# Delta rule: the two 64-token chunks of a block side by side, each on its own quarter of the array

## What is computed

```python
gc = jnp.cumsum(g, axis=-1)                       # within a chunk
decay = jnp.exp(jnp.where(causal, gc[..., :, None] - gc[..., None, :], -jnp.inf))
lower = jnp.where(strict, jnp.einsum('bhnid,bhnjd->bhnij', kb, k) * decay, 0.0)
tmat = lax.linalg.triangular_solve(eye + lower, ...)   # inverse of eye + lower, 64 x 64
u = jnp.einsum('bhnij,bhnjd->bhnid', tmat, v * beta[..., None])
w = jnp.einsum('bhnij,bhnjd->bhnid', tmat, kb * jnp.exp(gc)[..., None])
a_intra = jnp.where(causal, jnp.einsum('bhnid,bhnjd->bhnij', q, k) * decay, 0.0)
def step(S, inp):                                 # one chunk after another
    v_new = ui - wi @ S
    o = (qi * exp(gci)) @ S + ai @ v_new
    S = S * exp(glast) + (ki * exp(glast - gci)).T @ v_new
```

## Time and profile before

| | |
|---|---|
| runs | 3397.33, 3400.24, 3403.83 us |
| span of the profiled execution, first to last instruction | 3398.0 us |
| TensorE busy in the span | 3301.7 us (97%) |
| first pair: heads, inversion, state | 22.6, 30.2, 21.9 us |
| second pair: heads, inversion, state | 25.1, 31.7, 21.8 us |

### The profile page before, as it was taken

The page is one execution under the profiler, slowest core; times in us unless marked ns, Lnnn a source line. Parts: engine busy times, 40 slices in busy tenths (PEclk is TensorE's granted clock), DMA queues, the critical chain, the costliest instruction groups (busy, mean ns, idle before and its releaser), DMA issues. The chain is left out here.

```text
span 3398.0 us, 46483 instructions
## 1 busy us (share of the span) xinstructions
PE 3301.7 (97%) x18292; PEld 3053.0 (90%) x18292; DVE 2275.5 (67%) x3841; ACT 1235.4 (36%) x2071; POOL 80.7 (2%) x190
## 2 busy tenths in 40 slices
PE   8999999999999999989999999989999999999999
PEld 6999999988899999989999999977888888888777
DVE  5979896467677777787777766664333766466654
ACT  5111112256553433363433343543222432334432
POOL 0000000000000000000000000000000000000100
PEclk9999999999999999999999999999999999999999
DMA  5545553200132222232232221112233320122232
GB/s 209 186 168 180 191 176 110 73 26 26 42 88 67 87 87 79 90 84 65 73 100 87 93 87 61 44 61 87 94 100 95 124 63 20 54 78 74 69 100 94
DMA packets 95272, 313.57 MB, mean 92 GB/s; under 512 B 11424, under 2 KB 15712, under 8 KB 93520
## 3 DMA queue, kind: packets, MB, share of 16 engines
q1 hardware_dynamic: 88128, 290.04, 25.9%
q0 software_dynamic: 6928, 20.55, 2.2%
HBM read 300.06 MB, written 4.19 MB: 90 GB/s over the span
## 5 line engine op out<-in xcount | busy, mean ns | idle before, releaser
L669 PE MATMUL psum<-zh,wh 128*128 128x384 f32 (+2 forms) x2384 | 777.1, 371 | 24.3 <-DVE h L752 5.7
L639 ACT ACTIVATE wh<-raw 128x512 fp32r<-128x512 f32 (+3 forms) x551 | 447.4, 817 | 836.3 <-PE psum L669 431.9
L669 PE MATMUL psum<-zh,rawl 128*128 128x384 f32 (+2 forms) x2384 | 750.9, 360 | 0.0
L669 PE MATMUL psum<-zl,wh 128*128 128x384 f32 (+2 forms) x2372 | 747.6, 360 | 0.0
L649 DVE TENSOR_TENSOR rawl<-raw,wh 128x512 fp32r<-128x512 f32 (+3 forms) x551 | 502.6, 927 | 242.9 <-ACT wh L639 241.6
L669 PEld LDWEIGHTS psum<-zh,wh 128*128 128x128 f32 x2384 | 439.5, 190 | 79.5 <-issue 25.5
L1135 PE MATMUL psum<-formq,wh 128*128 128x386 f32 x1848 | 479.7, 341 | 10.9 <-DVE made_l L649 4.1
L669 PEld LDWEIGHTS psum<-zh,rawl 128*128 128x128 f32 x2384 | 441.2, 190 | 43.0
L669 PEld LDWEIGHTS psum<-zl,wh 128*128 128x128 f32 x2372 | 438.9, 190 | 41.5 <-issue 2.9
L1135 PEld LDWEIGHTS psum<-formq,wh 128*128 128x128 f32 x1848 | 337.5, 189 | 16.5 <-DVE made_l L649 5.0
L752 DVE SCALAR_TENSOR_TENSOR h<-psum,mod,h 128x512 f32<-128x512 f32 (+1 forms) x288 | 170.0, 627 | 190.7 <-PE psum L669 190.6
(11 more groups left out here) (494 smaller groups left out, 4747.7 us busy)
## 6 DMA issues: line engine op xcount, KB each, us to landing
raw<-in_wup SPq DMA_DIRECT2D x176, 512.0 KB, 4.1
modw<-in_mod_w SPq DMA_DIRECT2D x128, 512.0 KB, 3.7
raw<-in_w_sw SPq DMA_DIRECT2D x36, 512.0 KB, 3.6
raw<-in_wdn SPq DMA_DIRECT2D x64, 256.0 KB, 3.9
raw<-in_wdn SPq DMA_DIRECT2D x32, 448.0 KB, 3.2
adaw<-in_ada_w SPq DMA_DIRECT2D x8, 1024.0 KB, 15.0
raw<-in_wdn SPq DMA_DIRECT2D x16, 512.0 KB, 4.0
raw<-in_od_in SPq DMA_DIRECT2D x16, 512.0 KB, 3.6
```

Of the source, the lines that this page charges most:

```text
L639: nc.scalar.activation(hi_of(n, i), x, ACT.Copy).then_inc(w_hi, 1)
L669: last = nc.tensor.matmul(psum[:, at + to:at + to + e - s], w[:, q * P:(q + 1) * P], x[:, q, s:e], start=(q == 0 and j == 0), stop=(q == s ...
```

## The change

Wherever a matrix over pairs of tokens is block diagonal, only the two 64 by 64 chunks are kept: chunk 0 in partitions 0 to 63 and chunk 1 in partitions 64 to 127, both in columns 0 to 63 (`C`) of the same buffers. Each product becomes two (`for r in CHUNKS`), one for each chunk. In the inversion both operands and the result of a chunk lie in its own 64 partitions, so chunk 0 uses rows and columns 0 to 63 of TensorE's array and chunk 1 rows and columns 64 to 127. KK, KQ and BET contract over all 128 rows and write 64 output partitions each. The transpose of `uu` becomes a product with the identity. The w products write the two row halves into two banks (XB and UB), and ScalarE gathers them. ScalarE and VectorE work on 64 of 128 columns per head. `at_` stays 128 by 128; its zeros are set once. The mask constant keeps its size and is laid out anew. In `dn_head_pe` the row sums in chunk form are a further product, beside BET in the same bank.

```diff
@@ -3098,7 +3098,15 @@
             pool.wait_ge(n_sum, 7)
             pool.dma_start(dmask[:], t["c_dmask"]).then_inc(dmask_loaded, 16)
 
-        MASKT, CUM, BLK = dmask[:, 0, :], dmask[:, 1, :], dmask[:, 2, :]
+
+
+        C = slice(0, 64)
+        CHUNKS = (slice(0, 64), slice(64, 128))
+        CUM, BLK = dmask[:, 1, :], dmask[:, 2, :]
+        MASKT, IDENT = dmask[:, 0, C], dmask[:, 0, 64:128]
+
+        def level_mask(lv):
+            return mid(dmask[:, 3 + lv, C], 4)
 
...
@@ -3127,12 +3135,19 @@
                 w(dd, "lt", a - 1)
             for hd in range(4):
                 nc.tensor.matmul(bank4(ROW)[:, hd], buf["xx"][:, hd], CUM, start=True, stop=True)
-                last = nc.tensor.matmul(bank4(BET)[:, hd], buf["uc"][:, hd], ident[:], start=True, stop=True)
+            for hd in range(4):
+                for r in CHUNKS:
+                    nc.tensor.matmul(bank4(BET)[r, hd, 64:128], buf["xx"][:, hd, C], CUM[:, r], start=True, stop=True)
+                for r in CHUNKS:
+                    last = nc.tensor.matmul(bank4(BET)[r, hd, C], buf["uc"][:, hd, C], ident[:, r],
+                                            start=True, stop=True)
             last.then_inc(dp.sem, 1)
             for hd in range(4):
                 q, k = dn[:, hd, tok], dn[:, 4 + hd, tok]
-                nc.tensor.matmul(bank4(KK)[:, hd], k, k, start=True, stop=True)
-                last = nc.tensor.matmul(bank4(KQ)[:, hd], k, q, start=True, stop=True)
+                for r in CHUNKS:
+                    nc.tensor.matmul(bank4(KK)[r, hd, C], k[:, r], k[:, r], start=True, stop=True)
+                for r in CHUNKS:
+                    last = nc.tensor.matmul(bank4(KQ)[r, hd, C], k[:, r], q[:, r], start=True, stop=True)
             last.then_inc(dp.sem, 1)
             if a % 2:
                 w(dd, "vb", a - 1)
@@ -3151,7 +3166,9 @@
                 if a % 2 == 0:
                     w(dd, "et", a + 1)
                 for hd in range(4):
-                    last = nc.tensor.transpose(bank4(ROW + a % 2)[:, hd], dnbs[a % 2]["uu"][:, hd], ident[:])
+                    for r in CHUNKS:
+                        last = nc.tensor.matmul(bank4(ROW + a % 2)[r, hd, C], dnbs[a % 2]["uu"][r, hd, C], ident[r, r],
+                                                start=True, stop=True)
                 last.then_inc(dp.sem, 1)
             for lv in LV:
                 for a in pair:
@@ -3162,8 +3179,9 @@
                     else:
                         w(dd, f"tt{lv - 1}", a)
                     for hd in range(4):
-                        last = nc.tensor.matmul(bank4(XB[a % 2])[:, hd], buf["uc"][:, hd], buf["tt"][:, hd],
-                                                start=True, stop=True)
+                        for r in CHUNKS:
+                            last = nc.tensor.matmul(bank4(XB[a % 2])[r, hd, C], buf["uc"][r, hd, C],
+                                                    buf["tt"][r, hd, C], start=True, stop=True)
                     last.then_inc(dp.sem, 1)
                 for a in pair:
                     buf = dnbs[a % 2]
@@ -3171,21 +3189,26 @@
                     if lv > 1:
                         w(dd, f"tu{lv - 1}", a)
                     for hd in range(4):
-                        last = nc.tensor.matmul(bank4(UB[a % 2])[:, hd], buf["xx"][:, hd], buf["uu"][:, hd],
-                                                start=True, stop=True)
+                        for r in CHUNKS:
+                            last = nc.tensor.matmul(bank4(UB[a % 2])[r, hd, C], buf["xx"][r, hd, C],
+                                                    buf["uu"][r, hd, C], start=True, stop=True)
                     if lv < 5:
                         for hd in range(4):
-                            last = nc.tensor.matmul(bank4(TB[a % 2])[:, hd], buf["uu"][:, hd], buf["xx"][:, hd],
-                                                    start=True, stop=True)
+                            for r in CHUNKS:
+                                last = nc.tensor.matmul(bank4(TB[a % 2])[r, hd, C], buf["uu"][r, hd, C],
+                                                        buf["xx"][r, hd, C], start=True, stop=True)
                     last.then_inc(dp.sem, 1)
             for a in pair:
                 buf = dnbs[a % 2]
                 w(dd, "tu5", a)
                 for hd in range(4):
-                    nc.tensor.matmul(bank4(TB[a % 2])[:, hd], buf["uu"][:, hd], buf["vb"][:, hd],
-                                     start=True, stop=True)
-                    last = nc.tensor.matmul(bank4(XB[a % 2])[:, hd], buf["kbe"][:, hd], buf["uu"][:, hd],
-                                            start=True, stop=True)
+                    for r in CHUNKS:
+                        nc.tensor.matmul(bank4(TB[a % 2])[r, hd], buf["uu"][r, hd, C], buf["vb"][r, hd],
+                                         start=True, stop=True)
+                    for half in CHUNKS:
+                        for b, r in zip((XB, UB), CHUNKS):
+                            last = nc.tensor.matmul(bank4(b[a % 2])[half, hd, C], buf["kbe"][r, hd, half],
+                                                    buf["uu"][r, hd, C], start=True, stop=True)
                 last.then_inc(dp.sem, 1)
...
@@ -3269,19 +3292,20 @@
                     w(dp, "ws1", a - 2)
                 run(buf["wt"][:], bank4(ROW), ACT.Exp)
                 w(dd, "et", a)
-                run(buf["et"][:], buf["et"][:], ACT.Exp)
+                run(buf["et"][:, :, C], buf["et"][:, :, C], ACT.Exp)
                 fill(HEADS[1 + a % 2])
             for a in pair:
                 w(dp, "ut", a)
-                run(dnbs[a % 2]["tt"][:], bank4(ROW + a % 2))
+                run(dnbs[a % 2]["tt"][:, :, C], bank4(ROW + a % 2)[:, :, C])
             for lv in LV:
                 for a in pair:
                     w(dp, f"x{lv}", a)
-                    run(dnbs[a % 2]["xx"][:], bank4(XB[a % 2]))
+                    run(dnbs[a % 2]["xx"][:, :, C], bank4(XB[a % 2])[:, :, C])
             for a in pair:
                 w(dp, "uw", a)
                 nc.scalar.activation(dnbs[a % 2]["xx"][:], bank4(TB[a % 2]), ACT.Copy)
-                run(dnbs[a % 2]["wt"][:], bank4(XB[a % 2]))
+                by_chunk = psum[:, XB[a % 2] * 512:(XB[a % 2] + 2) * 512].rearrange("p (g h n) -> p h g n", g=2, h=4)
+                run(dnbs[a % 2]["wt"].rearrange("p h (g n) -> p h g n", g=2), by_chunk[:, :, :, C])
             for a in pair:
                 for _ in range(4):
                     fill(STATE)
...
@@ -3315,7 +3339,7 @@
                 w(dp, "row", a)
                 w(da, "er", a)
                 for hd in range(4):
-                    last = nc.vector.scalar_tensor_tensor(buf["et"][:, hd], bank4(ROW)[:, hd],
+                    last = nc.vector.scalar_tensor_tensor(buf["et"][:, hd, C], bank4(BET)[:, hd, 64:128],
                                                           dncol[:, sm, hd:hd + 1], MASKT, ALU.subtract, ALU.add)
                 done(last, "et", a)
                 nc.vector.tensor_copy(dncol[:, sm + 2, 0:8].rearrange("p (h s) -> p h s", h=4),
@@ -3323,22 +3347,25 @@
                 tt(buf["qe"][:], dn[:, 0:4, tok], buf["wt"][:], ALU.mult).then_inc(dd.sem, 1)
                 w(da, "et", a)
                 w(dp, "kk", a)
-                link(dve, "dve", tt(buf["lt"][:], buf["et"][:], bank4(BET), ALU.mult))
-                tt(buf["at_"][:], buf["et"][:], bank4(KQ), ALU.mult)
-                done(tt(buf["lt"][:], buf["lt"][:], bank4(KK), ALU.mult), "lt", a)
+                lt, et = buf["lt"][:, :, C], buf["et"][:, :, C]
+                link(dve, "dve", tt(lt, et, bank4(BET)[:, :, C], ALU.mult))
+                for r in CHUNKS:
+                    tt(buf["at_"][r, :, r], et[r], bank4(KQ)[r, :, C], ALU.mult)
+                done(tt(lt, lt, bank4(KK)[:, :, C], ALU.mult), "lt", a)
                 w(dp, "tm", a)
                 tt(buf["vb"][:], bank4(VT), bc(b4, full), ALU.mult)
                 tt(buf["kbe"][:], bank4(KT), bc(dncol[:, sm + 1, 8:12], full), ALU.mult)
                 tt(buf["ke"][:], bank4(KT), bc(dncol[:, sm + 1, 4:8], full), ALU.mult).then_inc(dd.sem, 1)
-                link(dve, "dve", tt(buf["uc"][:], buf["lt"][:], mid(dmask[:, 3, :], 4), ALU.mult))
-                done(tt(buf["uu"][:], mid(ident[:, :], 4), buf["uc"][:], ALU.subtract), "u1", a)
-                tt(buf["uc"][:], buf["lt"][:], mid(dmask[:, 4, :], 4), ALU.mult).then_inc(dd.sem, 1)
+                uc = buf["uc"][:, :, C]
+                link(dve, "dve", tt(uc, lt, level_mask(0), ALU.mult))
+                done(tt(buf["uu"][:, :, C], mid(IDENT, 4), uc, ALU.subtract), "u1", a)
+                tt(uc, lt, level_mask(1), ALU.mult).then_inc(dd.sem, 1)
                 fill(HEADS[1 + a % 2])
             for lv in LV:
                 if lv < 5:
                     for a in pair:
                         w(dp, f"x{lv}", a)
```

(20 more changed lines are left out.)

## The result

The changed kernel takes 3372.61 us (median of 4 runs, 3364.18 to 3374.06), the kernel before 3399.54 us on the same chip (median of 4, 3397.33 to 3403.83). The ratio of the paired runs is 0.9915, with a 95% interval of 0.9903 to 0.9927: faster by 0.85%, and by 26.9 us between the two medians, where 10.3 us were forecast. The profiled execution spans 3371.1 us and took 3372.87.

The account below looks back on a forecast made before the run. TensorE's issue of products was taken to bound the inversion. New passes 60.8 us, plus 2.0 for changes of shape, less 69.5 removed and 3.6 of waits and clock, gave -10.3: from 3400.2 to 3390 us, range 3374 to 3416.

Parts of the forecast that it names:

- levels: Inversion, 224 new 64 by 64 passes per block, 896 in all, at 0.042 us replacing 448 at 0.1115: -12.3 us.
- u and w: Products after the inversion: 128 w passes at 0.042 us and 64 u passes costing 4.4 us, replacing 64: +2.6 us.
- heads: BET, KK, KQ and the transpose before each inversion: 320 new passes at 0.042 us less 12.4 removed, +1.0 us.
- changes of shape: TensorE switching product shape in heads and around the inversion: 12 changes at 0.17 us, +2.0 us, at most 4.1.
- waits and clock: TensorE's waits for dn_uu shrink, saving 2.9 us, and half of 1.3 us lost at low clock returns: -3.6 us.
- the price of a pass: New 64 by 64 passes on TensorE: 0.042 us with overlapping quarters, between 0.029 and 0.058, using L1754's 0.03 us step.
- Serial price: A 64 by 64 pass on TensorE that waits for the one before: 0.058 us.
- Rival (2): No overlap: passes in the inversion and w products queue at 0.058 us; +13 us, 3413; chance 0.24.
- Rival (3): Instruction stream is the floor: 0.061 us per load-and-product pair whatever its shape, as in L1570; +17 us, 3417; chance 0.14.
- Rival (1): Quarters overlap fully, passes at 0.029 us, 4 us bare in 10 levels: -24.6 us, 3376; chance 0.50 together with the forecast.
- TensorE bounds, not the copies: Inversion in the kernel before: TensorE busy 30.2 of 30.2 and 31.7 of 31.7 us, so its issue of products bounds.
- VectorE's operations and the two memsets: Shorter VectorE operations in the heads; at_ memsets (0.485 us each) before the first pair hidden, otherwise costing 1 us.

Follow-up runs that it names:

- Levels by chunk: Changed kernel with the levels' products reordered, all four heads of chunk 0, then all of chunk 1: 3377.53 us, ratio 0.9931 to the kernel before.
- heads by chunk: Changed kernel with BET, KK and KQ reordered, all heads of chunk 0, then all of chunk 1: ratio 0.9917 to the kernel before.
- one quarter: Changed kernel with both products of each pair in the levels on chunk 0's quarter, chunk 1's left out: 3414.87 us, ratio 1.0042 to the kernel before.
- t first: Changed kernel with t's product issued ahead of u's in levels 1 to 4, with its own signal: 3367.86 us, on another chip 3368.5 us.
- narrow copies alone: Kernel before, products kept at 128 by 128, ScalarE's and VectorE's work in the levels at half width: 3397.0 us against 3401.09, ratio 0.9989.

## Why the prediction was wrong

The direction and the mechanism held: TensorE's issue of products bounded the inversion, and the quarters run side by side. The size was off by 17 us (26.9 against 10.3), and the time fell 1.4 us under the range's low end. By stages, with the prediction's own terms:

| us | forecast | measured | what it was |
|---|---|---|---|
| levels | 896 x 0.042 - 448 x 0.1115 = -12.3 | -23.5 | 896 x 0.0292 + 4.0 bare, from 50.0 + 2.2 bare + 1.5 clock |
| u and w | 128 x 0.042 + 4.4 - 64 x 0.1115 = +2.6 | -1.7 | 96 passes of a pair in 2.84 us |
| heads | 320 x 0.042 - 12.4 = +1.0 | | 320 x 0.0292 - 12.4 = -3.1 |
| changes of shape | +2.0 | | about +1.2 |
| waits and clock | -3.6 | | -2.5 wait; the clock's part is the 1.5 in the first row |
| heads with these two | | -4.1 | -3.1 + 1.2 - 2.5 = -4.4, 0.3 too much |
| sum | -10.3 | -29.1 (state +0.2) | |

- **The step that failed** is the price of a pass in "I take that: (58 + 26 to 30)/2 = 0.042 to 0.044, price 0.042". A pass cost 0.0292 us on average: the step to another quarter costs nothing, not 0.03 us. That is 1344 x (0.042 - 0.0292) = 17.2 us. I had the bound that came true ("from below by nothing") and chose by the nearest row, L1754, whose eight products are one stream of full height and say nothing on two quarters. "Levels by chunk" and "heads by chunk" show that the price hangs on what runs beside a pass, "one quarter" that it is 0.058 with nothing beside it.
- **Serial price** of 0.058 from the earlier trace rows: right to the digit (0.93 us for 16). Rival (2) is what the "one quarter" kernel does: 26 us in the levels of pair one. It decides only where the second quarter stands still.
- **Rival (3)**, 0.061 whatever the shape: excluded. Two passes start every 0.058 us, on average 0.029 apart. What holds L1570 at 0.061 was not tested.
- **Rival (1)** at 3376 was the true case, with its bare 0.4 us per level (measured 0.41: (15.12 - 448 x 0.0292)/5). The prediction did not say where in the level they lie; they are for the most part the wait for VectorE's `tt`, and in "t first", without that wait, 0.28 is left. It said -24.6 where the delta rule gave -29.1; the u and w products came out cheaper than its 7.2 us by 1.5, and the levels of before had 2.2 us of hand-over that the sum of passes did not hold. I put it at the edge of the forecast instead of in its middle, so the range ended where the likeliest case lay.
- **"TensorE bounds, not the copies"** was right for the kernel before up to 1.1 us per pair (narrow copies alone), which "30.2 of 30.2 us" busy did not show: a product is listed as 0.275 us long where the next starts 0.1115 us later, its end is modelled, and so it covers a short hand-over.
- **Changes of shape**: ROW's last product starts at 2783.98 and BET's first at 2784.18, 0.20 us instead of the regular 0.11; L669 at 2799.04, L3170 at 2799.36, instead of 0.23. About 0.1 us each, not 0.17: 1.2 us, if the other ten of the twelve are like these two. The row that I used, L3218, leaves another shape.
- **Waits**: 3.9 to 1.4 us, forecast 3.9 to 1.0. **Clock**: in the kernel before it was low behind the 2.7 us wait; in the changed one that stretch is gone, all of its 1.5 us and not the 0.65 that I counted. A second stretch of 3.4 us at 0.50, near the start of the heads of pair two, I overlooked. It is in both kernels, so it cancels in the difference (23.40 us against 21.8 in four of the kernels run, which have no such stretch). Where the low clock falls varies from run to run, and one time (3364.18) had a mean clock of 0.995 where the others had 0.991 or 0.992. The heads of pair two in the kernel before, to be put beside the window from 2840.60 of the changed one above:
```profile
2851.70:2877.30 25.60, 22.85 (x142) 20.48 (x143) 17.42 (x36) 5.69 (x13) 0.00 (x0) 0.93 0.14 42
```
- **VectorE's operations and the two memsets** lay beside other work, as said: state +0.08 us per pair, no wait for at_.

## What to carry to other kernels

When a block-diagonal product is split over two quarters of the array, count the passes of the busier quarter at their serial price and take the other quarter's as free: 0.0292 us on average here, for halves of rows and for halves of columns alike; but keep the order alternating, at most four passes on one quarter in a row. Half the size at twice the count is worth nothing by itself (26.05 us, as before), and once the passes are cheap the copies between them have to shrink with them, or they are the next bound (17.7 against 15.1 us). Where a term of the sum can lie anywhere between two ends and no row shows the resource, work out the time at both ends and let the range reach beyond the end, rather than taking the middle from a row of another kind; and read an edit's effect from its own stages, since the clock can move the total by as much as a small edit does (3372.61 and 3368.73 us for the same kernel, at mean clocks of 0.991 to 0.992 and of 0.994).

## What was not expected of the hardware

- Products of a quarter that is free start ahead of earlier ones of a busy quarter (L3193 at 2801.39, before L3183 at 2801.44). A run of four passes on one quarter is hidden whole (15.1 us), one of eight in part (18.2 us, where no overlap gives 26.05).
- In the "one quarter" kernel the granted clock fell 1.9 us after the levels of pair two had begun. Ahead of them TensorE was busy 2.21 of 3.60 us, still at 1.00. The clock then stayed at its lower level (1.2 GHz) until 2923.2 us, 47.8 us in all (mean 0.52 over the levels), through unbroken work on one quarter. In pair one the same work began at the higher level, behind a stretch with TensorE busy 3.50 of 3.60 us, and kept it for 26.0 us. The changed kernel had the same stretch ahead of its levels of pair two (2.20 busy of 3.60 us) and kept 1.00 behind it, with both quarters at work. The clock rose again once the u and w products and full-size ones ran (0.61 over 2917 to 2925). So neither the stretch ahead nor the work on one quarter lowered the clock by itself; what did, and why the one quarter's work did not raise it again, is open.
